# Causal convolution taps moved from TensorE to ScalarE and GpSimd in a two-layer hybrid block

## The chip, the cores and the metric

One core of a Trainium2 chip runs the whole kernel. The metric is the device time of one execution in microseconds, given as the median of several runs. The engines are TensorE (PE), VectorE (DVE), ScalarE (ACT), GpSimd (POOL) and the DMA queue of SyncE (SP). All of them run their own list of instructions in order and wait for each other through semaphores that are written out by hand.

## What is computed

The input is a sequence of 256 tokens with 1024 features. Two blocks of two layers each follow one another. The change touches the first block alone; its layer is, cut to what matters:

```python
a = rmsnorm(h, norm_mix_pre[i])
u = einsum('bsd,de->bse', a, w_in[i])
q, k, v, qi, ki, wi, u_conv, u_pool = split(u, IN_SPLITS)
# index scores: sum over 16 heads of relu(qi . ki) * wi; the 64 best keys of each token are kept
idx = einsum('bths,bth->bts', relu(einsum('bthd,bsd->bths', qi, ki)), wi) * idx_scale
_, sel = top_k(where(causal, idx, -inf), 64)
# softmax attention of 8 heads over the kept keys
# convolution branch, 256 channels, 31 causal taps
a, g = split(u_conv, 2)
y = a * sigmoid(g)
y = depthwise_conv(y, conv_dw, kernel=31) + conv_b
y = silu(layernorm(y, ln_g, ln_b)) @ conv_pw
# pooling branch: windowed means of 2, 4, 8, 16 tokens, minus the token, times pool_w, pool_scale
mix = concatenate([y_attn, y_conv, y_pool]) @ w_out
h = h + rmsnorm(mix, norm_mix_post)
# then a feed-forward part and a gated embedding
```

The second block (feed-forward, recurrent and retention mixer, feed-forward) is the same before and after.

## The kernel before

Weights arrive in chunks of 128 partitions by 2048 floats (1 MB), each as two half chunks of 1024 columns. SP loads a half chunk into one of two raw slots (`raw`) when VectorE has finished with the chunk two places earlier. ScalarE rounds it (`prep`, line 490, tile `whi`), VectorE subtracts to get the low part (`lo`, line 946, tile `wlo`), and TensorE multiplies three times (high by high, high by low, low by high). There are four places for such pairs, so ScalarE also waits until TensorE has released the chunk four places earlier. `prep(s)` and `lo(s)` stand at fixed places of their engines' lists and bring all chunks up to s.

A layer of the first block uses chunks 0 to 10 of its own for the input projection, and 11 to 14 for the output product. In the old order they are: 0 and 1 keys, values and index keys; 2 to 5 the index queries (`qi`), two of 8 heads each; 6 and 7 the queries (`q`); 8 and 9 the convolution's inputs and gates, one group of 128 channels each; 10 the pooling's input. The functions `block_in` (512 columns, 12 products for four feature tiles) and `pair_in` (256 columns, 24 products for a half chunk) do them, lines 1780 and 1826.

TensorE turns the projected tiles to feature-major form (`turn_in`, line 1797) once VectorE has applied the rotation (`rope`, line 1059); ScalarE copies the turned tiles out of PSUM (`turned_in`, line 573). Then come the index products (`dots`, line 1819), sixteen heads; two heads whose operands lie in different partition halves run side by side on TensorE when they are issued one after the other. ScalarE applies relu (line 590), VectorE multiplies by the weight and sums (`index_sums`, line 1084), three buffers deep. After the last head VectorE searches: eight rounds of MAX8 and MATCH_REPLACE8 (lines 1130, 1133). Then it copies the pooling input (line 1138), makes the additive mask `bias` (lines 1142 to 1145) and masks the scores of head after head (`masked`, lines 1152, 1156). ScalarE takes the exponential (line 637), TensorE turns the probabilities (`turn_probs`, 1889), ScalarE copies them (645), and TensorE multiplies by the values (`mix_values`, 1901 to 1905).

The convolution has two groups of 128 channels and 31 taps, 62 in all. Forty-six of them are done on TensorE (`taps`, line 1927): the product of a diagonal matrix of the tap's weights with the shifted input `YC`, in plain float32, which the trace records as two passes each. GpSimd makes the diagonals (line 415) in a ring of 16. The last 16 taps of group 1 are done by VectorE (`own_taps`, lines 1184, 1186) in the softmax stage, and added through one product with the identity (line 1945). TensorE does 14 taps before the first head and 7, 7, 6, 6, 6 after the first five. ScalarE then adds the convolution's bias (line 661); mean, variance and the scale follow as products with a constant matrix (lines 1951, 1966, 1975). GpSimd also does the pooling sums (lines 427 to 441) between two groups of diagonals. At the end the output product begins with the first half of the values (`tail`, line 1668, with `last_values` after one chunk).

At the start of the kernel, ScalarE and VectorE also make the sines of the rotation: VectorE `angles_by_feature` (line 1029) between `lo(2)` and `lo(3)`, ScalarE `sines` (line 521) after `prep(2)`.

## Time and profile before

| | us |
|---|---|
| median of 3 runs | 2367.45 |
| lowest, highest | 2366.25, 2367.78 |
| the profiled execution, its own time | 2367.65 |
| its span, first to last instruction | 2365.9 |
| TensorE busy | 2338.3 (99%) |
| VectorE busy | 1550.9 (66%) |
| ScalarE busy | 1195.0 (51%) |
| GpSimd busy | 119.3 (5%) |

Busy time is the time in which an engine has an instruction under way. Products overlap on TensorE, so what counts for its list is the distance from start to start. A timeline row gives the start, the time from the start of the first to the end of the last of the merged instructions, the engine, the line, what was written and read, the shape and the count, and in brackets the idle time before it with what ended it. The profile's lines are those of the kernel printed above.

### The profile page before, as it was taken

How to read it: one execution, taken by the hardware profiler on the slowest of the kernel's cores; microseconds unless marked ns; L12 is line 12 of the kernel's file. 1: busy time of each engine (PE TensorE's matmuls, PEld its weight loads, DVE VectorE, ACT ScalarE, POOL GpSimd, SP SyncE). 2: the span in 40 equal slices, each digit the busy share in tenths (PEclk: the TensorE clock that was granted, in tenths of full speed). 3: DMA queues.
4: the chain of work that ended last, by engine and by line, in shares of the span. 5: the costliest groups of instructions: out<-in, count | busy, mean ns of one | idle time of the engine just before them, and what ended most of it. 6: DMA issues, size and time to landing. Idle time of an engine off the chain costs nothing.

```text
span 2365.9 us, 30405 instructions
## 1 busy us (share of the span) xinstructions
PE 2338.3 (99%) x12096; PEld 1979.0 (84%) x12096; DVE 1550.9 (66%) x2041; ACT 1195.0 (51%) x1734; POOL 119.3 (5%) x223
## 2 busy tenths in 40 slices
PE   7999999999999999999999999999999999999998
PEld 6888888888888888988888888888889888888887
DVE  6866567866666656776485666665567765856664
ACT  6445446445455546546344455554465553444553
POOL 0500000500000000000000000000000000000000
PEclk9999999999999999999999999999999999999999
DMA  7236656236556665554656465565565455564553
GB/s 270 83 104 205 205 190 214 72 107 213 186 176 227 196 196 179 196 167 160 199 174 202 161 211 181 178 229 197 181 196 194 159 168 188 182 207 162 191 193 125
DMA packets 117501, 427.11 MB, mean 181 GB/s; under 512 B 13296, under 2 KB 13552, under 8 KB 117104
## 3 DMA queue, kind: packets, MB, share of 16 engines
q1 hardware_dynamic: 117360, 425.16, 54.4%
q8 instruction: 97, 1.59, 0.3%
q14 instruction: 44, 0.36, 0.0%
HBM read 424.05 MB, written 1.05 MB: 180 GB/s over the span
## 4 chain that ended last, share of the span: by engine, by line
PE 87%; DVE 6%; POOL 2%; DMA 1%; ACT 1%; issue 1%; SPq 0%; DVEq 0%; POOLq 0%; ACTq 0%
PE ub L1625 21%; PE ub L1626 11%; PE ub L1610 8%; PE ub L1612 8%; PE ub L1611 8%; PE acc L1610 8%; PE acc L1612 7%; PE acc L1611 7%; DVE wlo L946 2%; DMA raw<-in_w 1%; DVE XN L987 1%; PE acc L1927 1%; POOL tapd L415 1%; ACT junk L512 1%; PE acc L2040 1%
## 5 line engine op out<-in xcount | busy, mean ns | idle before, releaser
L946 DVE TENSOR_TENSOR wlo<-raw,whi 128x1024 fp32r<-128x1024 f32 x776 | 917.4, 1223 | 243.8 <-ACT whi L490 241.3
L490 ACT ACTIVATE whi<-raw 128x1024 fp32r<-128x1024 f32 x776 | 783.1, 1053 | 258.5 <-PE ub L1612 149.0
L1625 PE MATMUL ub<-xhl,whi 128*128 128x512 f32 x2176 | 770.3, 398 | 0.0
L1626 PE MATMUL ub<-xhl,wlo 128*128 128x256 f32 x2176 | 609.7, 280 | 0.0
L1625 PEld LDWEIGHTS ub<-xhl,whi 128*128 128x128 f32 x2176 | 408.6, 188 | 98.7 <-issue 0.5
L1626 PEld LDWEIGHTS ub<-xhl,wlo 128*128 128x128 f32 x2176 | 410.7, 189 | 2.4 <-issue 0.5
L1610 PE MATMUL acc<-whi,bhl 128*128 128x512 f32 x736 | 289.5, 393 | 0.0
L1612 PE MATMUL acc<-whi,bhl 128*128 128x512 f32 x736 | 287.1, 390 | 0.0
L1611 PE MATMUL acc<-wlo,bhl 128*128 128x512 f32 x736 | 286.8, 390 | 0.0
L1610 PE MATMUL ub<-whi,xhl 128*128 128x512 f32 (+1 forms) x704 | 275.4, 391 | 9.3 <-DVE wlo L946 5.0
L1612 PE MATMUL ub<-whi,xhl 128*128 128x512 f32 (+1 forms) x704 | 272.5, 387 | 0.0
L1611 PE MATMUL ub<-wlo,xhl 128*128 128x512 f32 (+1 forms) x704 | 272.3, 387 | 0.0
L1610 PEld LDWEIGHTS ub<-whi,xhl 128*128 128x128 f32 x704 | 132.7, 189 | 38.5 <-DVE wlo L946 7.2
L1612 PEld LDWEIGHTS acc<-whi,bhl 128*128 128x128 f32 x736 | 138.1, 188 | 29.9
L1610 PEld LDWEIGHTS acc<-whi,bhl 128*128 128x128 f32 x736 | 138.2, 188 | 29.0
L1611 PEld LDWEIGHTS acc<-wlo,bhl 128*128 128x128 f32 x736 | 138.3, 188 | 27.0
L1612 PEld LDWEIGHTS ub<-whi,xhl 128*128 128x128 f32 x704 | 132.6, 188 | 26.6
L1611 PEld LDWEIGHTS ub<-wlo,xhl 128*128 128x128 f32 x704 | 132.8, 189 | 25.3
L1348 DVE TENSOR_TENSOR tX<-tS,ub 128x512 f32<-128x512 f32 x72 | 49.5, 688 | 140.4 <-ACT tS L773 139.9
L773 ACT ACTIVATE tS<-ub 128x512 f32<-128x512 f32 x72 | 43.0, 597 | 154.3 <-PE ub L1626 154.1
L1610 PE MATMUL ub<-whi,bhl 128*128 128x512 f32 x256 | 99.8, 390 | 0.0
L1612 PE MATMUL ub<-whi,bhl 128*128 128x512 f32 x256 | 99.6, 389 | 0.0
(311 smaller groups left out, 2577.7 us busy)
## 6 DMA issues: line engine op xcount, KB each, us to landing
raw<-in_w SPq DMA_DIRECT2D x776, 512.0 KB, 4.8
gain<-in_gains SPq DMA_DIRECT2D x20, 512.0 KB, 8.1
par<-in_par SPq DMA_DIRECT2D x2, 1068.0 KB, 9.2
DEC<-in_decay SPq DMA_DIRECT2D x2, 768.0 KB, 7.5
H<-in_x SPq DMA_DIRECT2D x2, 512.0 KB, 6.2
out_h<-H SPq DMA_DIRECT2D x4, 256.0 KB, 2.3
par<-in_par SPq DMA_DIRECT2D x2, 419.0 KB, 7.9
PT<-in_p SPq DMA_DIRECT2D x2, 256.0 KB, 8.1
```

Of the source, the lines that this page charges most:

```text
L415: do(pool.tensor_scalar(tapd[:, n % TAP_RING, :], ident, par1[:, P1["dw"] + n:P1["dw"] + n + 1], 1.0, ALU.mult, ALU.mult), taps)
L490: do(act.activation(whi[:, s % RING, c], raw[:, s % RAW, c], ACT.Copy), counts["w_hi"])
L512: do(act.activation(junk[:, :], H[:, t, fcol(fb)], ACT.Square, scale=1.0 / 32, accum_out=ssh[:, t, fb:fb + 1]), counts["ssh"])
L773: do(act.activation(units(tS[:, j % 2, :]), ub[:, 2 * (j % 2):2 * (j % 2) + 2, 0:S], ACT.Copy), counts["a_out"])
L946: do(dve.tensor_tensor(wlo[:, s % RING, c], raw[:, s % RAW, c], whi[:, s % RING, c].bitcast(f32), ALU.subtract), counts["w_lo"])
L987: do(dve.scalar_tensor_tensor(XN[:, fcol(fb)], H[:, t, fcol(fb)], rh[:, t:t + 1], gain[:, 1, fcol(fb)], ALU.mult, ALU.mult), counts["xn_re ...
L1348: do(dve.tensor_tensor(units(tX[:, j % 2, :]), units(tS[:, j % 2, :]), ub[:, 2 * (j % 2):2 * (j % 2) + 2, S:2 * S], ALU.add), counts["us"])
L1610: pe.matmul(o, x_h, w_h, start=first, stop=False, skip_group_check=True)
L1611: pe.matmul(o, x_h, w_l, start=False, stop=False, skip_group_check=True)
L1612: return pe.matmul(o, x_l, w_h, start=False, stop=last, skip_group_check=True)
L1625: pe.matmul(bank, w_h, x.rearrange("p a n -> p (a n)"), start=first, stop=False, skip_group_check=True)
L1626: return pe.matmul(bank[:, S:], w_l, x[:, 0, :], start=False, stop=last, skip_group_check=True)
```

## The change

The 62 taps are divided anew. Group 0: tap 0 with the bias and all 30 others are made as products on ScalarE (`first_tap`, `tap_products`) and summed on GpSimd into `cacc`. Group 1: taps 0 to 10 are done that way too, tap 0 on ScalarE and ten as products on GpSimd itself; eight (11 to 18) stay on TensorE, with diagonals made early and kept apart (no ring); the last twelve stay on VectorE. ScalarE writes into a ring of four slots `prods` and waits for GpSimd's add of the product four places earlier. GpSimd adds group 0 alone for the first twenty products (256 elements) and both groups at once for the last ten (512 elements).

The chunks change places: 6 and 7 are the convolution's, 8 and 9 the queries, 10 the pooling's. The index products begin after the first half of chunk 4. The turn of the first index queries comes right behind that of the keys. The queries' rotation comes after the search, the pooling input's copy behind six of VectorE's own taps and chunk 11's low part. At the start chunks 3 and 4 are prepared ahead of the sines and `angles_by_feature`. Scores are issued two heads at a time. The pool product moves behind the last head, and the convolution's scale and output products move by some places in the output product.

```diff
-TAP_RING = 16
+TAP_RING = 4
-TAPS_DVE = 16
-TAPS_BEFORE, TAPS_AFTER = 14, (7, 7, 6, 6, 6)
+TAPS_POOL, TAPS_PE, TAPS_DVE = 11, 8, 12
+TAPS_BEFORE = 4
+TAP_ORDER = tuple(range(TAPS_POOL, TAPS)) + tuple(range(1, TAPS_POOL))
...
+        tapd = sb("tapd", 0, at=place[0], shape=[P, TAPS_PE, P])
+        prods = sb("prods", 0, at=unit(32), shape=[P, TAP_RING, 2, S])
...
GpSimd
-                    pool.wait_ge(sem["dots_done"], IDX_HEADS * (L + 1))
-                    early = TAP_RING + TAPS_BEFORE
-                    tap_diagonals(0, early)
+                    for n in range(TAPS_PE):
+                        c = P1["dw"] + TAPS + TAPS_POOL + n
+                        do(pool.tensor_scalar(tapd[:, n, :], ident, par1[:, c:c + 1], 1.0, ALU.mult, ALU.mult),
+                           counts["tap_ready"])
+                    for n, k in enumerate(TAP_ORDER):
+                        pool.wait_ge(sem["tap_made"], (TAPS + 1) * L + 1 + n + 1 + (k < TAPS_POOL))
+                        x = prods[:, n % TAP_RING, :, :]
+                        if k < TAPS_POOL:
+                            c = P1["dw"] + TAPS + k
+                            do(pool.tensor_scalar(x[:, 1, :], YC[:, 1, k:k + S], par1[:, c:c + 1], 1.0, ALU.mult, ALU.mult))
+                            settle()
+                            do(pool.tensor_tensor(cacc[:, :, :], cacc[:, :, :], x, ALU.add), counts["tap_used"])
+                        else:
+                            settle()
+                            do(pool.tensor_tensor(cacc[:, 0, :], cacc[:, 0, :], x[:, 0, :], ALU.add), counts["tap_used"])
                     nxt("pool_in")
...
-                    tap_diagonals(early, 2 * TAPS - TAPS_DVE)
...
ScalarE
                 prep(2)
                 sines_by_token()
+                prep(4)
                 sines()
...
+                    def first_tap(f):
+                        act.wait_ge(sem["in_free"], 3 * L + f + 1)
+                        act.wait_ge(sem["par_in"], 16 * (L + 1))
+                        do(act.activation(cacc[:, f, :], YC[:, f, 0:S], ACT.Identity,
+                                          bias=par1[:, P1["conv_b"] + f:P1["conv_b"] + f + 1],
+                                          scale=par1[:, P1["dw"] + f * TAPS:P1["dw"] + f * TAPS + 1]), counts["tap_made"])
+                    def tap_products(first, end):
+                        for n in range(first, end):
+                            if n == TAPS - TAPS_POOL:
+                                first_tap(1)
+                            if n >= TAP_RING:
+                                act.wait_ge(sem["tap_used"], (TAPS - 1) * L + n - TAP_RING + 1)
+                            k = TAP_ORDER[n]
+                            do(act.activation(prods[:, n % TAP_RING, 0, :], YC[:, 0, k:k + S], ACT.Copy,
+                                              scale=par1[:, P1["dw"] + k:P1["dw"] + k + 1]), counts["tap_made"])
...
+                    prep(s0 + 7)
                     turned_in(0)
+                    turned_in(1)
+                    relus(0, 2)
                     prep(s0 + 8)
+                    relus(2, 5)
                     copy(2, 0)
                     copy(2, 1)
-                    turned_in(1)
+                    relus(5, 8)
                     prep(s0 + 9)
-                    relus(0, 4)
+                    turned_in(2)
+                    sigmoid(0)
+                    relus(8, 11)
+                    first_tap(0)
+                    tap_products(0, 4)
                     prep(s0 + 10)
-                    turned_in(2)
-                    relus(4, 10)
+                    relus(11, 14)
+                    tap_products(4, 6)
+                    sigmoid(1)
+                    relus(14, 16)
+                    tap_products(6, 10)
                     prep(s0 + 11)
+                    tap_products(10, 14)
                     copy(3, 0)
+                    tap_products(14, 18)
                     copy(3, 1)
-                    relus(10, 13)
-                    sigmoid(0)
-                    relus(13, 16)
                     prep(s0 + 12)
-                    sigmoid(1)
-                    prep(s0 + 13)
+                    tap_products(18, 24)
                     turned_in(3)
+                    tap_products(24, TAPS - 1)
...
VectorE
-                lo(2)
+                lo(4)
                 angles_by_feature()
-                lo(3)
...
+                    rope(1)
+                    lo(s0 + 7)
+                    index_sums(0, 2)
                     lo(s0 + 8)
+                    index_sums(2, 5)
                     rope(2)
+                    index_sums(5, 8)
                     lo(s0 + 9)
-                    index_sums(0, 4)
-                    lo(s0 + 10)
-                    index_sums(4, 10)
-                    lo(s0 + 11)
-                    rope(3)
-                    index_sums(10, 16)
                     dve.wait_ge(sem["pads_ready"], L + 1)
                     gated(0)
+                    index_sums(8, 11)
+                    lo(s0 + 10)
+                    index_sums(11, 14)
+                    gated(1)
+                    index_sums(14, 16)
...
-                        if r == 3:
-                            gated(1)
-                    used(s0 + 10)
-                    do(dve.tensor_copy(UP[:, :, 16:], units(acc[:, 2, :])), counts["in_free"])
...
+                    rope(3)
                     settle()
                     do(dve.tensor_scalar(bias[:, :], cur, TAKEN, OFF, ALU.not_equal, ALU.mult))
...
+                    lo(s0 + 11)
+                    dve.wait_ge(sem["par_in"], 16 * (L + 1))
+                    own_taps(TAPS - TAPS_DVE, TAPS - TAPS_DVE + 6)
+                    used(s0 + 10)
+                    do(dve.tensor_copy(UP[:, :, 16:], units(acc[:, 0, :])), counts["in_free"])
...
                     masked(0)
                     masked(1)
                     lo(s0 + 12)
                     for hh in range(HEADS):
                         if hh + 2 < HEADS:
                             masked(hh + 2)
-                        if hh < 4:
+                        if hh < 3:
+                            k0 = TAPS - TAPS_DVE + 6 + 2 * hh
+                            own_taps(k0, k0 + 2)
...
+                        if hh == 5:
+                            nxt("conv_done")
+                            dve.wait_ge(sem["tap_used"], (TAPS - 1) * (L + 1))
+                            do(dve.tensor_tensor(cacc[:, 1, :], cacc[:, 1, :], acc[:, 3, S:2 * S], ALU.add), counts["c_ready"])
...
TensorE
-                    both(2, 0)
+                    block_in(2, 0, 0)
                     turn_in(0)
-                    both(2, 1)
                     turn_in(1)
-                    block_in(3, 0, 0)
+                    give(block_in(2, 0, 1))
                     dots(0, 2)
+                    give(block_in(2, 1, 0), "xz")
+                    dots(2, 5)
+                    give(block_in(2, 1, 1))
+                    dots(5, 8)
+                    pair_in(s0 + 6, 2, 0)
                     turn_in(2)
+                    pair_in(s0 + 6, 2, 1)
+                    dots(8, 11)
+                    pair_in(s0 + 7, 0, 0)
+                    dots(11, 14)
+                    pair_in(s0 + 7, 0, 1)
+                    dots(14, 16)
+                    for part in range(2):
+                        both(3, part)
+                    pair_in(s0 + 10, 0, 0)
                     turn_in(3)
+                    pair_in(s0 + 10, 0, 1)
...
                     scores(0)
                     scores(1)
-                    taps(TAPS_BEFORE)
+                    taps(0, TAPS_BEFORE)
                     for hh in range(HEADS):
                         turn_probs(hh)
-                        if hh + 2 < HEADS:
+                        if hh % 2 == 0 and hh + 2 < HEADS:
                             scores(hh + 2)
+                            scores(hh + 3)
                         if hh:
                             mix_values(hh - 1)
-                        if hh < len(TAPS_AFTER):
-                            taps(TAPS_AFTER[hh])
+                        if hh < TAPS_PE - TAPS_BEFORE:
+                            taps(TAPS_BEFORE + hh, TAPS_BEFORE + hh + 1)
...
                     mix_values(HEADS - 1)
+                    pe.wait_ge(sem["par_in"], 16 * (L + 1))
+                    nxt("pool_out")
...
```

## Rows read from the trace of the kernel before

**Rows 1.** Windows: us; busy of PE, PEld, DVE, ACT, POOL; PEclk, DMA share, GB/s

```profile
...
427.50:441.10 13.60, 13.60 (x104) 12.79 (x103) 12.74 (x54) 4.53 (x6) 5.41 (x15) 1.00 0.01 2
441.10:476.90 35.80, 34.89 (x193) 28.32 (x193) 31.70 (x56) 14.97 (x46) 23.91 (x35) 1.00 0.28 89
...
```

**Rows 2.** Timeline of PE, second layer: start us, duration us, what [idle before]

```profile
...
457.60 2.17 PE L1927 MATMUL acc<-YC,tapd 128*128 128x256 f32 x8 [0.91 <-POOL tapd L415]
...
461.60 2.81 PE L1927 MATMUL acc<-YC,tapd 128*128 128x256 f32 x12
464.25 0.49 PE L1889 MATMUL ub<-cst,sm 128*128 128x128 f32 x3
...
476.93 0.48 PE L1610 MATMUL acc<-whi,bhl 128*128 128x512 f32 x1
...
```

**Rows 3.** Timeline of DVE, second layer, index sums to the first scores

```profile
...
424.11 2.60 DVE L1084 SCALAR_TENSOR_TENSOR iacc<-sm,wi,iacc 128x128 f32<-128x128 f32 x6 [0.46 <-ACT sm L590]
...
427.30 0.62 DVE L1130 MAX8 best<-iacc 128x8 f32<-128x128 f32 x2
...
428.74 0.62 DVE L1130 MAX8 best<-work 128x8 f32<-128x128 f32 x2
...
439.22 0.68 DVE L1138 COPY UP<-acc 128x512 f32<-128x512 f32 x1
...
441.11 0.56 DVE L1152 SCALAR_TENSOR_TENSOR sm<-ub,bias 128x384 f32<-128x384 f32 x1
...
443.55 2.35 DVE L946 TENSOR_TENSOR wlo<-raw,whi 128x1024 fp32r<-128x1024 f32 x2
```

**Rows 4.** Timeline of DVE, second layer, softmax stage

```profile
...
448.00 2.88 DVE L1186 SCALAR_TENSOR_TENSOR CD<-YC,par,CD 128x256 f32<-128x256 f32 x3
...
459.73 2.09 DVE L1186 SCALAR_TENSOR_TENSOR CD<-YC,par,CD 128x256 f32<-128x256 f32 x4
...
471.29 0.61 DVE L1156 TENSOR_REDUCE rmax<-sm 128x1 f32<-128x128 f32 x2
...
```

**Rows 5.** Timeline of POOL, second layer, softmax stage

```profile
...
446.73 1.08 POOL L427 TENSOR_TENSOR W<-UP 128x542 f32<-128x542 f32 x1
...
449.05 0.69 POOL L431 TENSOR_TENSOR W<-W 128x265 f32<-128x265 f32 x1
...
457.01 8.84 POOL L415 TENSOR_SCALAR tapd<-cst,par 128x128 f32<-128x128 f32 x16
```

**Rows 6.** Tile tapd: min/median/max ns of one, first and last start

```profile
...
L415 POOL TENSOR_SCALAR tapd<-cst,par x92: 366/374/2509, 76.7 to 464.5; 128x128 f32<-128x128 f32 x92
...
```

**Rows 7.** Timeline of PE, second layer: turns of keys and of index queries

```profile
...
390.93 0.60 PE L1804 MATMUL ub<-cst,Z 128*128 128x128 f32 x4
...
396.86 1.03 PE L1811 MATMUL ub<-cst,ZA 128*128 128x128 f32 x8
...
```

**Rows 8.** Timeline of DVE, second layer: end of their rotation

```profile
...
390.88 0.43 DVE L1077 TENSOR_TENSOR ZA<-tX 128x256 f32<-128x256 f32 x1
...
```

**Rows 9.** Timeline of PE, second layer: conv half chunk, products of 256 columns

```profile
...
415.45 0.28 PE L1617 MATMUL acc<-xhl,whi 128*128 128x256 f32 x1
...
415.81 0.28 PE L1617 MATMUL acc<-xhl,whi 128*128 128x256 f32 x1
...
```

**Rows 10.** Timeline of PE, start of the kernel

```profile
...
15.41 0.48 PE L1612 MATMUL ub<-whi,xhl 128*128 128x336 f32 x1
...
16.96 0.32 PE L1612 MATMUL ub<-whi,xhl 128*128 128x336 f32 x1
...
31.48 0.50 PE L1610 MATMUL ub<-whi,xhl 128*128 128x512 f32 x1 [1.79 <-DVE wlo L946]
...
```

**Rows 11.** Timeline of DVE, first layer: angles, then lo of chunk 3

```profile
...
24.96 0.35 DVE L1033 TENSOR_SCALAR ang<-posf,cst 128x256 f32<-128x256 f32 x1
...
30.20 2.36 DVE L946 TENSOR_TENSOR wlo<-raw,whi 128x1024 fp32r<-128x1024 f32 x2 [1.74 <-ACT whi L490]
...
```

135 lines of the change are left out of this document (47 added, 88 removed).

## The prediction

> **What bounds the kernel now.** The page says TensorE 99% busy, so I read first where the change works: two stretches, one in each layer of the first block (about 37 to 129 us and 385 to 477 us), that repeat almost to the tenth. The windows [rows 1] show in the second layer 13.6 us of search in which TensorE is always busy and VectorE 12.74 of 13.6, and then a softmax stage of 35.8 us with TensorE at 34.9 and VectorE at 31.7. So TensorE ends last, but VectorE has only 4.1 us to spare in that stage. Next, TensorE's timeline [rows 2]: six taps (12 records, two passes each) fill 461.60 to 464.25, so a tap is 0.442 us; once TensorE waits 0.91 us for a tap's diagonal; the output product starts at 476.93. Then VectorE's timeline [rows 3]: three heads of index sums in 2.45 us (0.82 a head, 2.60 with GpSimd at work), search from 427.30, one round in 1.44, its end where the pool copy begins at 439.22, masks from 441.11, two of them in 2.44 (1.24 with gaps), one chunk's low part in 2.35. In the stage itself [rows 4] four of its own taps take 2.09 (0.52 each) and the last reduction ends at 471.90, 5.0 before the output product.
>
> **What TensorE loses.** 38 of 46 taps a layer go: 38 x 0.442 = 16.8 us, with the 0.91 wait 17.7, twice 35.4. Scores by pairs spare single-head products as well; I price them at nothing, because VectorE's list covers them, and if that cover went they would add to the gain. This saving counts only as far as the others follow, so the sum goes by them.
>
> **What GpSimd gets.** Twenty adds of 256 elements, ten more of 512, each of those with a product of 256. An add of 542 takes 1.08, one of 265 takes 0.69 [rows 5]: 1.4 ns an element on 0.31, so 0.68 and 1.04, plus 0.08 between dependent ones. The product of 256 is not in the trace; a 128-wide one takes 0.374 [rows 6], so between that and twice it; I take 0.50, nearest to the same start-up plus twice the data. Sum 20 x 0.76 + 10 x 1.70 = 32 us, and then the pooling, 10.3 (446.73 to 457.01). From the first product at 413 this ends by about 469 with its waits, before the pool product near 479: its length is covered by search and softmax. ScalarE's 32 products (a 256-wide one about 0.4) lie in its idle time, but its ring of four slots ties it to the adds: the first exponential stands behind product 30, so behind add 26. I put that at 450.3, and with 1.3 of table load at 452 where its mask is ready at 450.7. Small, and VectorE's low part covers it. VectorE's new wait for add 30 stands ahead of the mean's subtraction and the values' low part; the adds end near 458.5 and it comes at 473.7, so it costs nothing, and the two copies of ScalarE that it replaces (0.8) were waiting time. No DMA is added; SP's queue keeps its order.
>
> **What GpSimd takes from VectorE.** One diagonal took 2.51 instead of 0.37 [rows 6], beside two low parts; three VectorE taps beside GpSimd's adds took 2.88 instead of 1.56 [rows 4, 5]. But four taps beside diagonals of 0.54 each were not slowed (2.09) [rows 4, 5]. So operations of VectorE with two SBUF inputs and GpSimd's exclude each other, and only while data move (1.4 ns an element on GpSimd, about 1 ns on VectorE); the start-up overlaps. Masks, reductions and search rounds beside GpSimd kept their times. The Trainium skill, "SBUF — State Buffer", "SBUF: two separate sides", has it that the shared pair of ports is locked for the whole instruction and the other engine blocks fully. The unslowed four taps speak against the whole length; by whole locks I would get about 22 us more instead of 7.
>
> **The second layer, step by step.** I wrote the engines' lists side by side, each step starting where the one ahead of it and its wait end. The same table for the old order gives search at 427.6 and masks at 441.5, within 0.4 of the rows.
> Head: the queries' turn is now right behind the keys' turn; that was 6 us earlier (390.93 to 396.86, two blocks of 2.72 between) [rows 7]. Its rotation ends at 391.3 [rows 8], because two low parts stand ahead. TensorE, there at 388.8, waits 2.5.
> Dots: behind the last dot stood two convolution half chunks (48 products every 0.12, 5.8 us [rows 9]) too many, now four query blocks: the pool's and the turn are common, so dots end 10.9 - 5.8 = 5.1 earlier less the 2.5: 2.6 earlier, 421.5.
> Index sums: eight heads, chunk 10's low part and the second gate now run against the adds; I count 2.7 of exclusion. Search starts at 425.9, 1.4 early, and ends 11.5 later at 437.4, since a gate is no longer in it.
> Then, ahead of the masks: the query rotation 1.35 (formerly while VectorE waited for dots), bias 1.05, low part 2.35, six taps 3.3, pool copy 0.85, together 8.9, and 3.0 of exclusion: first mask at 449.3, 8.2 later than 441.11. The scores are there at 444, so TensorE then stands idle.
> Stage: VectorE's masks 8 x 1.24 = 9.9, three low parts 7.1, six taps 3.1, the first half's division 1.1, exclusion 3.1: 24.3 to the last reduction (30.8 in the old order). Then exponential, last two heads, mean, square and variance products and now the pool product: 6.2 against 5.0. Output product at 479.8, **2.9 late**. TensorE's idle time there is some 19 us, in gaps of 7, 4.5 and 3.5.
>
> **The first layer.** Moving chunks 3 and 4 ahead of the angles removes the 1.79 wait [rows 10]: chunk 3 came behind the angles, begun at 24.96, at 30.20 [rows 11]. But the angles (3.9) now stand behind chunk 4's low part, which waits for its load and ends near 32; then sines, the copies and the first rotation end near 38.7, and the second one, behind chunk 5, at 42.4. TensorE waits 1.1 for the keys' turn, 3.2 for the queries', and 2.4 before the first dots, since ScalarE copies the turned data behind chunk 7: 6.7 for 1.8 and 0.6 now. Dots end as before; search starts about 0.5 later, the masks 10 later (103.1 for 93.4), and the stage is 5.9 shorter: **4.3 late**. The other chunks' order leaves each queue's load count as it was, loads one chunk behind their old place in the search are not needed before the output product: nothing.
>
> **Sum and median.** +2.9 + 4.3 = +7.2. The clock: after 7 us without work some of TensorE's next products may run at the lower level. At the start a 336-wide one takes 0.48, once it has worked 0.32 [rows 10]; the granted-clock column reads 1.00 in the stage now [rows 1], so no row shows a fall. Between 0 and all products of the stage doubled (5.5 a layer on the chain, and 1.4 on the output's first products) I take 1 a layer, as most of them wait for VectorE anyway. Total +9.2. The profiled execution took 2367.65 (span 2365.9 and 1.7 around it), 0.2 over the median 2367.45. Forecast **2377 us**. I call 0.2%, 4.7 us, what a measurement can tell.
>
> **Rivals.**
> 1. Forecast, 2377: VectorE is the stage's bound; chance 0.40, of which 0.16 within 0.2%.
> 2. Faster. The exclusion costs VectorE nothing and the head's turns find their rotations done. My count without these gives -4.9 in the second layer and -3.5 in the first: **2359**. For it: VectorE drops four taps a layer (2.1 us) and TensorE's 35 us are real. Against: three taps in 2.88. It decides if VectorE's delays fall under 5 us of my 8.8 a layer. Chance 0.26, 0.02 of it within 0.2%.
> 3. GpSimd is the bound: adds 30% dearer in data (0.87 for 256, toward the 0.79 of contended ones and beyond) put the exponentials behind the ring, +4.7 a layer: **2386**, chance 0.12.
> 4. TensorE falls to 1.2 GHz through the stage: 6.9 a layer on 7.2, **2388**, chance 0.16, 0.02 within. For it: gaps of 7 us. Against: work between them. The Trainium skill, "TensorE: Matmul & The Clock Gate", "What's actually happening", says an idle array is put back to half rate; no row here shows it after warm work.
> 5. Exclusion for whole instructions: +9.7 and +12.6 from my table so locked, **2390**, chance 0.06; the old order would then be some 13 us a layer slower than it is.
>
> The range: 2360 to 2392 leaves out about half of rival 2 and the tails of 4 and 5. Faster 0.24, the same 0.16 + 0.02 + 0.02 = 0.20, slower 0.56.
>
> **What the profile would show.** Right: TensorE's busy time in each softmax stage near 18 of 30 us, gaps before the first transposed head, first masks near 103 and 449, VectorE's low parts and taps slower than 1.18 and 0.52, waits before both first turns. Wrong: first masks before 445, or TensorE's gaps ended by GpSimd, or index sums beside adds at 0.82 a head, or a granted clock below 1.00 in the stage.

## The result, and the profile after

The kernel before took 2366.99 us (median of 6, 2366.2 to 2367.8), the changed one **2387.09** (median of 6, 2384.3 to 2391.0): ratio 1.0084, 95% interval 1.0074 to 1.0094, so 20 us slower. The forecast was 2377, in a range from 2360 to 2392. The profiled execution is the fastest of its six (2384.3, span 2382.5 for 2365.9), so the trace shows 16.6 us of those 20.

Where they are, by the starts on the timelines of VectorE and TensorE, in us (S first round of the search, M first mask, R last reduction, O output product):

| | S to M | M to R | R to O | S to O |
|---|---|---|---|---|
| before, both layers | 13.8 | 30.2 | 5.6 | 49.6 |
| after, first layer | 26.2 | 24.6 | 7.6 | 58.4 |
| after, second layer | 26.2 | 24.3 | 7.8 | 58.3 |
| forecast, second layer | 23.4 | 23.7 | 6.8 | 53.9 |

The search starts 0.9 later in the first layer (80.53 for 79.64) and, counted from the output product before it, 1.9 earlier in the second. So 0.9 + 8.8 = 9.7 in the first layer and 8.6 - 1.9 = 6.7 in the second: 16.4, nearly all there is. Behind the second output product both kernels take 1889 us. The 0.9 and the 1.9 are those of this one trace. In two kernels further down (e2, e4) the instructions ahead of each search, the head of the layer, are the same as here, and there the first search starts at 82.5 and 82.0, and the second comes 298.9 and 298.4 after the output product, for 296.1 here. Three traces of the old head (before, e6, e10) agree within 0.3 us: 79.3 to 79.6 and 298.0. So the new head varies by up to 2.0 us in the first layer and 2.8 in the second, and this trace, the fastest, flatters it. In e2's second layer ScalarE waits 2.08 us for a half chunk (1.05 here), VectorE's rotation of the first index queries stands behind that half chunk's low part, and TensorE waits for the rotation and then turns at the lower level. The turn in the changed kernel and in e2:

```profile
400.21 1.09 PE L1843 MATMUL ub<-cst,ZA 128*128 128x128 f32 x8 [1.65 <-DVE ZA L1104]
```

```profile
402.35 1.97 PE L1843 MATMUL ub<-cst,ZA 128*128 128x128 f32 x8 [2.93 <-DVE ZA L1104]
```

Windows of the changed kernel, second layer (columns as in [rows 1]):

```profile
435.00:447.00 12.00, 9.62 (x54) 8.27 (x52) 11.34 (x50) 9.59 (x20) 9.29 (x14) 1.00 0.00 1
461.00:494.00 33.00, 25.79 (x125) 20.79 (x126) 26.85 (x50) 17.00 (x47) 19.10 (x17) 0.69 0.30 96
```

TensorE is no longer full in either window, and its granted clock in the stage is 0.69: stretches at 1.2 GHz. The page's first part has VectorE 13 us and ScalarE 25 us busier, GpSimd 45, TensorE 14 less.

VectorE's timeline from the end of the search to the first mask (start, duration, what); where one instruction stands alone it was looked at in a narrow window:

```profile
446.10 0.41 DVE L1160 MATCH_REPLACE8 work<-best,work 128x256 f32<-128x256 f32 x1
446.62 0.46 DVE L1100 TENSOR_TENSOR tX<-ZA,cc 128x256 f32<-128x256 f32 x1
447.00 1.34 DVE L1101 TENSOR_TENSOR tX<-ZA,ss 128x128 f32<-128x128 f32 x1
...
449.12 1.31 DVE L1164 TENSOR_SCALAR bias<-work 128x384 f32<-128x384 f32 x1
...
451.04 3.44 DVE L974 TENSOR_TENSOR wlo<-raw,whi 128x1024 fp32r<-128x1024 f32 x2
454.59 0.35 DVE L1206 TENSOR_SCALAR CD<-YC,par 128x256 f32<-128x256 f32 x1
454.98 1.40 DVE L1208 SCALAR_TENSOR_TENSOR CD<-YC,par,CD 128x256 f32<-128x256 f32 x1
456.41 0.58 DVE L1208 SCALAR_TENSOR_TENSOR CD<-YC,par,CD 128x256 f32<-128x256 f32 x1
457.03 1.37 DVE L1208 SCALAR_TENSOR_TENSOR CD<-YC,par,CD 128x256 f32<-128x256 f32 x1
458.44 0.58 DVE L1208 SCALAR_TENSOR_TENSOR CD<-YC,par,CD 128x256 f32<-128x256 f32 x1
459.05 1.37 DVE L1208 SCALAR_TENSOR_TENSOR CD<-YC,par,CD 128x256 f32<-128x256 f32 x1
460.34 0.68 DVE L1215 COPY UP<-acc 128x512 f32<-128x512 f32 x1
...
461.26 0.56 DVE L1174 SCALAR_TENSOR_TENSOR sm<-ub,bias 128x384 f32<-128x384 f32 x1
```

and GpSimd's in the same stretch:

```profile
450.86 1.40 POOL L428 TENSOR_TENSOR cacc<-cacc,prods 128x512 f32<-128x512 f32 x1
452.24 2.51 POOL L426 TENSOR_SCALAR prods<-YC,par 128x256 f32<-128x256 f32 x1
454.83 1.27 POOL L428 TENSOR_TENSOR cacc<-cacc,prods 128x512 f32<-128x512 f32 x1
456.08 0.65 POOL L426 TENSOR_SCALAR prods<-YC,par 128x256 f32<-128x256 f32 x1
456.81 1.31 POOL L428 TENSOR_TENSOR cacc<-cacc,prods 128x512 f32<-128x512 f32 x1
458.10 0.65 POOL L426 TENSOR_SCALAR prods<-YC,par 128x256 f32<-128x256 f32 x1
458.83 1.31 POOL L428 TENSOR_TENSOR cacc<-cacc,prods 128x512 f32<-128x512 f32 x1
```

Lay the two side by side. The tap begun at 454.98 meets an add that lasts to 456.10 and ends 0.28 after it: 1.40 instead of 0.58. The next one meets a product and is not slowed; the one after it meets the next add, 1.37. And the other way round: GpSimd's product at 452.24 waits for the second piece of the low part, which ends at 454.48, and takes 2.51. So each engine stands still for most of the other's instruction, but for some 0.3 of start-up. The product shows it best: it began before VectorE's second piece (453.27), which passed it and was not slowed.

TensorE's timeline, the waits ahead of the query heads' turn, the first and the third transposed head, and the output product:

```profile
449.14 1.97 PE L1843 MATMUL ub<-cst,ZA 128*128 128x128 f32 x8 [4.52 <-DVE ZA L1104]
...
463.54 0.90 PE L1921 MATMUL ub<-cst,sm 128*128 128x128 f32 x3 [5.49 <-ACT sm L672]
...
470.88 0.81 PE L1921 MATMUL ub<-cst,sm 128*128 128x128 f32 x3 [2.02 <-ACT work L680]
...
493.31 0.58 PE L1642 MATMUL acc<-whi,bhl 128*128 128x512 f32 x1
```

The turn of eight took 1.97 here and 1.03 in [rows 7], the three transposes 0.81 to 0.90 for 0.49 [rows 2]: that is the lower level, behind waits of 4.5 and 5.5 us.

### The profile page after: what moved, and what is told of

The parts are those of the page before. It is cut to its first block, busy times and chain, and to the rows that moved or that the text cites. A ratio compares the mean times of both kernels' runs of the same rounds, so it can differ in the third digit from the quotient of the medians.

```text
span 2382.5 us, 30199 instructions
## 1 busy us (share of the span) xinstructions
PE 2323.9 (98%) x11944; PEld 1966.6 (83%) x11944; DVE 1564.2 (66%) x2035; ACT 1220.3 (51%) x1794; POOL 164.1 (7%) x227
## 3 DMA queue, kind: packets, MB, share of 16 engines
HBM read 424.05 MB, written 1.05 MB: 178 GB/s over the span
## 4 chain that ended last, share of the span: by engine, by line
PE 84%; DVE 10%; ACT 2%; DMA 2%; POOL 1%; issue 1%; DVEq 0%; SPq 0%; POOLq 0%; ACTq 0%
PE ub L1657 21%; PE ub L1658 11%; PE ub L1642 8%; PE ub L1644 8%; PE ub L1643 8%; PE acc L1642 7%; PE acc L1644 7%; PE acc L1643 7%; DVE wlo L974 3%; DMA raw<-in_w 2%; DVE CD L1208 1%; DVE XN L1015 1%; ACT whi L496 1%; ACT junk L518 1%; PE acc L2073 1%
## 5 line engine op out<-in xcount | busy, mean ns | idle before, releaser
L391 POOL TENSOR_SCALAR vy<-ssy 128x1 f32<-128x1 f32 x20 | 6.6, 332 | 1625.6 <-ACT junk L510 1625.6
L1642 PE MATMUL ub<-whi,bhl 128*128 128x512 f32 x256 | 99.8, 390 | 0.0
```

Source lines behind the costliest of these rows:

```text
L1642: pe.matmul(o, x_h, w_h, start=first, stop=False, skip_group_check=True)
```

## The experiments

The times in the first column are medians of 4 to 11 runs; the kernel before ran beside each of them at 2367.4 to 2367.7. All other columns are from one execution each, the profiled one, whose own time is in the second column and can lie some us from the median. The last column but one, the head, is the start of the first search and the time from the first output product to the second search. The other starts are those above, first / second layer:

| kernel | us | profiled | S to M | M to R | R to O | S to O | head | mean clock |
|---|---|---|---|---|---|---|---|---|
| before | 2367.0 | 2367.7 | 13.8 / 13.8 | 30.2 / 30.2 | 5.6 / 5.6 | 49.6 / 49.6 | 79.6 / 298.0 | 1.000 |
| after | 2387.1 | 2384.3 | 26.2 / 26.2 | 24.6 / 24.3 | 7.6 / 7.8 | 58.4 / 58.3 | 80.5 / 296.1 | 0.986 |
| e1 short adds | 2371.1 | 2369.2 | 20.0 / 20.0 | 24.7 / 23.6 | 9.5 / 7.0 | 54.3 / 50.6 | 78.9 / 294.4 | 0.990 |
| e2 TensorE filled | 2384.9 | 2387.1 | 26.3 / 26.3 | 24.3 / 24.3 | 6.7 / 6.7 | 57.2 / 57.2 | 82.5 / 298.9 | 0.995 |
| e3 ten taps to TensorE | 2377.1 | 2375.1 | 21.4 / 21.2 | 23.8 / 23.0 | 7.4 / 6.7 | 52.6 / 50.8 | 81.3 / 299.5 | 0.992 |
| e4 late taps | 2391.7 | 2393.4 | 21.2 / 20.7 | 32.3 / 32.4 | 7.3 / 8.1 | 60.8 / 61.1 | 82.0 / 298.4 | 0.983 |
| e6 before, eight taps | 2370.5 | 2370.2 | 14.5 / 14.5 | 28.8 / 28.8 | 8.0 / 7.5 | 51.3 / 50.8 | 79.3 / 298.0 | 0.987 |
| e7 turn later | 2387.6 | 2387.7 | 26.2 / 26.2 | 24.6 / 24.6 | 8.4 / 8.7 | 59.2 / 59.5 | 82.9 / 295.1 | 0.987 |
| e8 ring untied | 2372.3 | 2369.7 | 20.6 / 21.1 | 23.3 / 23.0 | 6.7 / 6.7 | 50.6 / 50.7 | 80.7 / 297.3 | 0.994 |
| e9 products on ScalarE | 2377.2 | 2377.6 | 23.4 / 22.3 | 24.0 / 24.0 | 6.7 / 7.9 | 54.0 / 54.2 | 82.0 / 296.7 | 0.992 |
| e10 eight taps, filled | 2376.6 | 2376.2 | 14.5 / 14.5 | 34.0 / 34.0 | 5.6 / 5.6 | 54.2 / 54.2 | 79.5 / 298.0 | 1.000 |
| e11 head | 2371.5 | 2372.5 | 21.6 / 21.5 | 23.2 / 23.2 | 6.7 / 6.7 | 51.4 / 51.4 | 78.7 / 300.3 | 0.992 |
| e12 late copy | 2372.2 | 2376.0 | 20.3 / 22.3 | 23.5 / 24.0 | 6.0 / 9.8 | 49.8 / 56.0 | 79.6 / 299.2 | 0.992 |
| e13 filled, the best | 2368.4 | 2370.2 | 19.6 / 22.1 | 22.7 / 22.7 | 7.5 / 6.0 | 49.8 / 50.8 | 80.4 / 298.0 | 0.997 |

**What the sums on GpSimd cost.**

```diff
-do(pool.tensor_tensor(cacc[:, :, :], cacc[:, :, :], x, ALU.add), counts["tap_used"])
+do(pool.tensor_tensor(cacc[:, :, 0:1], cacc[:, :, 0:1], x[:, :, 0:1], ALU.add), counts["tap_used"])
```

(the same for the add of one half and for GpSimd's product)

> The kernel after, in which GpSimd's thirty sums and ten products of the convolution work on one column instead of 256 (most of the convolution's sum is left out); every wait and every other instruction stays. Theory A, GpSimd's data phases cost VectorE its time: between the search's end and the first mask VectorE took 14.7 us where its operations alone would take 8.9, and in the stage its low parts and taps took 2.8 more than alone; so 8.4 us a layer come back, 2387 becomes about 2370, and the first masks come at about 101 and 450. Theory B, the order of work and the clock are what costs: VectorE's operations get shorter but the time stays over 2380. A time below 2366 would say that the sums cost more than their exclusion (the exponentials tied to them).

2371.11 (2367.6 to 2375.1), ratio to before 1.0017 [1.0008, 1.0026]: 16 of the 20 us came back, theory A's figure. Between the two profiled executions it is 15.1: 11.8 from S to O and 3.4 in the heads. The index sums no longer meet adds there, but 3.4 is also no more than what the heads vary by. VectorE's timeline from the search's end to the first mask in this kernel:

```profile
438.63 0.41 DVE L1160 MATCH_REPLACE8 work<-best,work 128x256 f32<-128x256 f32 x1
...
439.48 0.29 DVE L1101 TENSOR_TENSOR tX<-ZA,ss 128x128 f32<-128x128 f32 x1
...
440.46 0.36 DVE L1164 TENSOR_SCALAR bias<-work 128x384 f32<-128x384 f32 x1
...
441.30 2.35 DVE L974 TENSOR_TENSOR wlo<-raw,whi 128x1024 fp32r<-128x1024 f32 x2
...
444.14 2.59 DVE L1208 SCALAR_TENSOR_TENSOR CD<-YC,par,CD 128x256 f32<-128x256 f32 x5
...
447.56 0.56 DVE L1174 SCALAR_TENSOR_TENSOR sm<-ub,bias 128x384 f32<-128x384 f32 x1
```

The same list is 8.5 long (439.04 to 447.56) that took 14.7 beside the adds (446.51 to 461.26): 6.2 a layer in this stretch alone. The stage itself did not get shorter in the first layer (24.7) and little in the second (23.6), because the pooling now ran beside its first taps (pairs at 1.90 and 1.89, not shown) and TensorE stood at the lower level for much of it (a granted clock of 0.65 and 0.78 from M to O, R to O 9.5 and 7.0).

**What TensorE's lower level costs the changed kernel.** Identity products where TensorE waits, which nobody reads:

```diff
+for _ in range(30):
+    pe.transpose(ub[:, 2, 0:P], ident, ident)
 turn_in(3)
...
 for hh in range(HEADS):
+    if hh in (0, 2, 4):
+        fill_idle(42 if hh == 0 else 14)
     turn_probs(hh)
```

> The kernel after, with products of the identity on TensorE (30 ahead of the query heads' turn, 42 ahead of the first transposed head, 14 ahead of the third and of the fifth) where it otherwise waits; their results are never read. It should hold the granted clock at 1.00 through both softmax stages. Theory A, VectorE's list sets the stage and the clock costs 1 us a layer, in the tail behind the last reduction: about 2385. Theory C, the 1.2 GHz stretches are the missing 7 us and more: 2375 to 2379, with TensorE's products at their full rate. If the added products stand in the way of work, the gaps' ends get later and it is 2389 or more.

2384.88 (4 runs, 2384.6 to 2387.1), 2.2 below the changed kernel, as theory A had it, though with the changed kernel's runs 6.7 apart the medians alone would not show it. In the traces S to O is 57.2 for 58.3 and 58.4, nearly all of it behind the last reduction (6.7 for 7.6 and 7.8). The profiled execution as a whole is 2.8 slower, since its heads took 2.0 and 2.8 longer. M to R did not move by more than 0.3: there TensorE has room even at 1.2 GHz. The clock did not stay at 1.00 everywhere (0.995 in the mean for 0.986), so 1.1 a layer is the least that the level costs.

**Where VectorE's taps should be.**

```diff
-TAPS_POOL, TAPS_PE, TAPS_DVE = 11, 8, 12
-TAPS_BEFORE = 4
+TAPS_POOL, TAPS_PE, TAPS_DVE = 11, 18, 2
+TAPS_BEFORE = 12
...
-own_taps(TAPS - TAPS_DVE, TAPS - TAPS_DVE + 6)
...
```

> The kernel after, with ten of VectorE's twelve taps as products on TensorE (18 there, 2 on VectorE; 10 more diagonals for GpSimd before the first gate). TensorE has some 19 us idle per stage and 10 taps are 4.4 us. VectorE loses six taps of about 1 us ahead of the masks and four of 0.6 to 1.1 in the stage. Theory A (VectorE's list is the bound until the exponentials meet GpSimd's ring): masks are ready 6 us earlier, but the last product on ScalarE still waits for GpSimd's adds, so the first exponential moves by 1 us or less, and only the stage gets shorter: 4 to 5 us a layer, about 2378. If the ring does not hold it: 9 us a layer, 2369. Rival, TensorE's idle time is no room (the taps sit in the wrong places): 2384 or more.

2377.07 (8 runs, 2370.5 to 2384.0), as expected: S to M 5 us shorter, and then the ring holds. ScalarE's timeline in this kernel, and VectorE's first reduction, done at 455.84, after it:

```profile
454.59 0.51 ACT L625 ACTIVATE prods<-YC,par 128x256 f32<-128x256 f32 x1 [3.19 <-POOL cacc L433]
456.40 0.51 ACT L625 ACTIVATE prods<-YC,par 128x256 f32<-128x256 f32 x1 [1.30 <-POOL cacc L433]
458.21 0.51 ACT L625 ACTIVATE prods<-YC,par 128x256 f32<-128x256 f32 x1 [1.30 <-POOL cacc L433]
458.74 1.28 ACT L677 ACT_TABLE_LOAD   x1
460.03 0.40 ACT L677 ACTIVATE sm<-sm,rmax 128x128 f32<-128x128 f32 x1
```

```profile
455.23 0.61 DVE L1183 TENSOR_REDUCE rmax<-sm 128x1 f32<-128x128 f32 x2
```

The mask was ready 4.2 before its exponential (3.9 in the first layer): three products wait for three adds ahead of it. VectorE then waited 2.1 for TensorE's third scores, which stand behind that exponential.

**Taps behind the masks instead.** The six own taps and the low part of chunk 11 move behind the first masks, three taps behind each of heads 0 to 3.

```diff
-lo(s0 + 11)
-own_taps(TAPS - TAPS_DVE, TAPS - TAPS_DVE + 6)
...
-if hh < 3:
-    k0 = TAPS - TAPS_DVE + 6 + 2 * hh
-    own_taps(k0, k0 + 2)
+if hh < 4:
+    k0 = TAPS - TAPS_DVE + 0 + sum((3, 3, 3, 3)[:hh])
+    own_taps(k0, k0 + (3, 3, 3, 3)[hh])
```

> The kernel after, with VectorE's first six own taps and the low part of chunk 11 moved from ahead of the first masks to behind them (three taps behind each of the heads 0 to 3). Theory A: the first mask is ready 9 us earlier, but the exponentials stand behind GpSimd's ring (the last product on ScalarE at about 460 in the second layer) and VectorE's list keeps its length, so the end moves by 1 us or less a layer: 2385 to 2388. Rival, the late first mask itself is the cost (TensorE could work in the gap): 4 us a layer, 2379.

2391.72, 4 above the forecast's upper end. The order bought nothing, as expected, and lost what I had not seen. From the waits of VectorE in this kernel's second layer (who waited for whom: us in total, times, longest):

```profile
DVE UP L1213 <- PE acc L1649: 3.6, 1, 3.6
```

The taps had covered the time in which TensorE, held up by the query turn, makes the pool chunk that VectorE copies next.

**TensorE's saving by itself.** The kernel before, without 38 of its 46 taps and their diagonals:

```diff
-TAPS_BEFORE, TAPS_AFTER = 14, (7, 7, 6, 6, 6)
+TAPS_BEFORE, TAPS_AFTER = 4, (1, 1, 1, 1)
+TAP_LIST = [(0, 0)] + [(1, k) for k in range(7)]
...
-    early = TAP_RING + TAPS_BEFORE
+    early = 8
...
-tap_diagonals(early, 2 * TAPS - TAPS_DVE)
```

> The kernel before, in which TensorE does 8 taps a layer instead of 46 and GpSimd makes 8 diagonals (38 taps are left out of the convolution's sum; nothing takes their place). It prices TensorE's saving by itself. Theory A, the saving counts only as far as VectorE follows: from the first mask to the output product VectorE's list is 9.9 of masks, 7.1 of low parts, 8.4 of its sixteen taps, 1.1 for the division and about 1 of exclusion, 27.5, plus 5.6 behind the last reduction, 33.1 for 35.8 now: 2.7 us a layer, about 2362, less what a lower clock costs. Rival, TensorE's 16.8 us a layer count in full: 2334. Between, about 2350, if TensorE's load also delayed VectorE.

2370.46, ratio 1.0013 [1.0004, 1.0022]: the work was only taken away, and the kernel was slower, where theory A said 2362. Its window from the first mask to the output product of the second layer:

```profile
443.00:479.40 36.40, 32.76 (x122) 24.55 (x122) 29.82 (x57) 14.86 (x46) 8.68 (x8) 0.58 0.26 87
```

M to R fell from 30.2 to 28.8, R to O rose from 5.6 to 7.5 and 8.0, at a clock of 0.58 for 1.00 [rows 1]. TensorE with 38 of its taps gone is still 32.8 of 36.4 busy, since what is left takes nearly twice as long: with the taps out, the engine gets its first waits, and the lower level then fills it again.

The clock is only part of that loss. S to M is 14.5 for 13.8, and it is 14.5 as well in the next kernel, at a clock of 1.000. With most of the diagonals gone, GpSimd begins the pooling earlier, and its first add meets VectorE's mask. VectorE's instruction in the kernel before, and in this one beside GpSimd's add:

```profile
440.46 0.34 DVE L1144 TENSOR_TENSOR bias<-bias,cst 128x128 f32<-128x128 f32 x1
```

```profile
441.46 1.25 POOL L428 TENSOR_TENSOR W<-UP 128x542 f32<-128x542 f32 x1 [12.11 <-DVE small L1140]
...
441.80 1.06 DVE L1144 TENSOR_TENSOR bias<-bias,cst 128x128 f32<-128x128 f32 x1
```

From S to O the two layers together are 2.8 longer: 1.4 are this meeting, 4.2 the tails, and a gain of 2.8 from M to R stands against them.

**The same with TensorE kept busy.**

```diff
 taps(TAPS_BEFORE)
+fill_idle(36)
...
 taps(TAPS_AFTER[hh])
+fill_idle(16)
```

> The kernel before with 8 taps on TensorE and 38 left out (2370.5, its softmax stages at a granted clock of 0.50 to 0.72), now with identity products in their places that nobody reads: 36 ahead of the first transposed head and 16 behind each of the first five heads, about 2 us a head where the taps took 2.7. Theory C2, the lower level is what turned that kernel's saving into a loss: the clock stays at 1.00, the tail behind the last reduction falls from 7.5 back to 5.6, the stage gets to VectorE's list, so 2362 to 2364, faster than the kernel before. Rival, the loss has nothing to do with the clock (VectorE's own work is what is longer): 2370 again.

2376.58: a miss, because the filling was too much. TensorE's timeline of this kernel:

```profile
445.79 6.64 PE L1881 MATMUL acc<-cst 128*128 128x128 f32 x58
...
454.07 3.73 PE L1881 MATMUL acc<-cst 128*128 128x128 f32 x32
```

Sixteen took 3.7 us, more than the 2.7 of the taps they stood for, so M to R became 34.0 with TensorE full. It does show that the tail's loss is the clock: at 1.000 it is 5.6 again, and S to M stays at 14.5. Whether the thinned kernel would reach 2362 at the upper level stays open; I have no run with the right amount of filling.

**The head's order.**

```diff
-turn_in(1)
 give(block_in(2, 0, 1))
+turn_in(1)
```

> The kernel after with one move: the first query turn stands behind the second block of chunk 4 (2.7 us of products) instead of ahead of it. TensorE waited 3.15 us for it in the first layer and 1.65 in the second. If these waits are on the path to the search (TensorE's products end last before it): the search starts 1.5 to 2.5 earlier in the first layer and 1 to 1.5 in the second, and everything behind keeps its length, 2383 to 2385. Rival: VectorE's index sums beside GpSimd's adds end last, the search starts where it did, 2387.

2387.63 (4 runs, 2386.2 to 2389.8), level with the changed kernel. The second search came 1.0 earlier, counted from the output product before it; the first came 2.3 later and the tails 0.8 to 0.9 longer. The heads vary by as much without any edit (80.5 to 82.5, and 296.1 to 298.9), and the runs lie 4 to 7 us apart, so the 2 us looked for cannot be told; inconclusive.

**The ring untied** (on top of the ten taps):

```diff
-tap_products(24, TAPS - 1)
+tap_products(24, 27)
 exps(0)
+tap_products(27, 28)
 for hh in range(HEADS):
     if hh + 1 < HEADS:
         exps(hh + 1)
+    if hh < 2:
+        tap_products(28 + hh, 29 + hh)
```

> The kernel with ten of VectorE's taps on TensorE (2377), with ScalarE's last three tap products behind the first, second and third pair of exponentials instead of ahead of them all. There the first exponential came 5.1 us after its mask, behind GpSimd's adds. Theory A: it now comes 1.2 after the first mask, and the stage starts up to 5 us earlier; VectorE's operations run beside the adds for longer (1 to 2 us back), so 3 us a layer, about 2371. Rival, GpSimd's last sums become the bound at the mean (they end at 115 and 467, the mean's product is at 129 and 480): below 1 us a layer, 2375 or more.

2372.32, ratio 1.0020 [1.0011, 1.0030]; the first exponential 1.2 behind its mask in both layers (101.29 to 102.53, 449.59 to 450.83), so the ring no longer holds it. The median is 4.8 lower, 2.4 a layer of the 3 forecast, but the traces do not put that in the stage. S to O fell by 2.0 in the first layer and by 0.1 in the second, where M to R is 23.0 in both kernels. VectorE's wait for scores went from 2.1 to 1.2, and two of its low parts took 3.40 and 3.31 us beside the adds, for 3.31 and 2.55. The other 3 us between the two profiled executions are in the heads. What the traces place in the two stages is 2 us in all.

**The ten products on ScalarE** (on top of that):

```diff
+if k < TAPS_POOL:
+    do(act.activation(prods[:, n % TAP_RING, 1, :], YC[:, 1, k:k + S], ACT.Copy,
+                      scale=par1[:, P1["dw"] + TAPS + k:P1["dw"] + TAPS + k + 1]))
...
-do(pool.tensor_scalar(x[:, 1, :], YC[:, 1, k:k + S], par1[:, c:c + 1], 1.0, ALU.mult, ALU.mult))
```

> The previous kernel with the second half's ten tap products on ScalarE (0.42 us each) instead of GpSimd (0.65 each with its gap, one of them 2.5). GpSimd's pace for these ten taps falls from 2.0 to about 1.4 us each, its sums end some 7 us earlier, and VectorE's low part and taps meet less of it. Theory A: 1 to 2 us a layer beside the previous kernel, 2367 to 2369, level with the kernel before. Rival: ScalarE's extra 4.2 us stand ahead of the exponentials and take it back, 2371 or more.

2377.16, 4.8 slower, a miss. GpSimd's timeline of this kernel:

```profile
444.13 5.56 POOL L431 TENSOR_TENSOR cacc<-cacc,prods 128x512 f32<-128x512 f32 x4
452.08 4.60 POOL L431 TENSOR_TENSOR cacc<-cacc,prods 128x512 f32<-128x512 f32 x3 [2.40 <-ACT prods L626]
458.06 3.90 POOL L431 TENSOR_TENSOR cacc<-cacc,prods 128x512 f32<-128x512 f32 x2 [1.38 <-ACT prods L626]
```

The first four adds now follow each other without the product between them, exactly beside VectorE's rotation, three of whose four operations took 1.35 to 1.42 where one did in the previous kernel; then GpSimd stands empty behind ScalarE, which waits 3.4 for the query turn that this rotation holds up. Products between the adds were VectorE's gaps; that this is the whole loss is argued, not tested. It was not the rival that I had named: the first exponential starts at 456.20, with the end of its mask's reduction.

**Smaller repairs.** The chunk between the angles taken back:

```diff
-prep(4)
+prep(3)
...
-lo(4)
+lo(3)
```

> The kernel with ten taps on TensorE and the last three products behind exponentials (2372), with chunk 4 taken out from between the two sets of angles: only chunk 3 stands ahead of the second angles and the sines. In the first layer the angles stood behind chunk 4's low part, and TensorE waited 2.3, 3.2 and 2 us for turned data. Theory A: these waits get 1.5 to 2.5 shorter, once: 2370. Rival, TensorE then waits for chunk 4's low part behind the angles (as for chunk 3 in the kernel before, 1.8): 2372 or more.

2371.47 (2367.8 to 2375.3), 0.9 below; the keys' turn 1.5 earlier (38.94 for 40.48) and the first search 2.0 earlier, but S to M came out 0.4 to 1.0 longer and the second search 3.1 later. Within the spread; no more than the earlier turn is shown.

> The previous kernel with the pool copy behind the first two masks (VectorE waited 0.7 us for it there) and the pool's product ahead of the variance product instead of behind the last head. GpSimd takes the pool up only behind its sums, so the later copy delays nothing; the product (1.1 us) then stands where TensorE waits 0.5 us for ScalarE's squares. Theory: 0.7 and 0.5 to 1 a layer, 2 to 3 in all below the previous kernel, 2367 to 2368. Rival: the pool's result is not ready there (it ends at 474.7, the squares' product is at about 476 in the second layer), TensorE waits for GpSimd, and it is level or slower.

```diff
+masked(0)
+masked(1)
 used(s0 + 10)
 do(dve.tensor_copy(UP[:, :, 16:], units(acc[:, 0, :])), counts["in_free"])
...
-masked(0)
-masked(1)
```

(and the pool's product moved ahead of the variance product)

2372.24, from 2366.4 to 2376.0: no gain in the median. But its profile holds a good and a bad layer of one program, S to O 49.8 and 56.0. Windows from the last third of the first and of the second stage (they do not hold just the same products):

```profile
120.00:130.00 10.00, 10.00 (x61) 9.11 (x61) 6.25 (x16) 4.23 (x13) 5.18 (x7) 0.83 0.31 106
...
470.00:480.00 10.00, 10.00 (x44) 8.59 (x43) 5.23 (x12) 4.18 (x14) 4.30 (x4) 0.50 0.33 105
```

TensorE is full in both: 61 products at a clock of 0.83, 44 at 0.50. The ten runs of this kernel go with the mean clock: 0.996 in the fastest, 0.992 in the slowest (correlation -0.90; -0.96 in the eight runs of e3, from 2370.5 at 0.995 to 2384.0 at 0.989). Which of the two is cause a correlation does not say; the next kernel tests it.

**All of it, with TensorE's waits filled.**

```diff
+pe.wait_ge(*U_[1].free)
+for _ in range(14):
+    pe.transpose(ub[:, 1, 0:P], ident, ident)
 turn_in(1)
...
+for _ in range(34):
+    pe.transpose(ub[:, 2, 0:P], ident, ident)
 turn_in(3)
...
 for hh in range(HEADS):
+    for _ in range(8 if hh == 2 else 4 if hh == 4 else 0):
+        pe.matmul(acc[:, 3, 0:P], ident, ident, start=False, stop=False, skip_group_check=True)
     turn_probs(hh)
```

> The previous kernel (2372.2, runs from 2366.4 to 2376.0; in its profile the first layer takes 49.8 us from the search to the output product at a clock mostly 1.00 and the second 56.0 with 0.50 in its last third), with products of the identity where TensorE waits: 14 ahead of the first query turn (1.6 us), 34 ahead of the query heads' turn (3.9 of a 4.5 us wait), 8 of two passes ahead of the third transposed head (1.9 of 2.3) and 4 ahead of the fifth (0.9 of 1.3). Theory C3: the spread of these kernels is where TensorE's lower level falls; with the waits filled the clock stays at 0.998 or more, both layers take 49.5 to 50.5, and it is 2367 to 2369 with runs within 3 us, level with the kernel before. Rival: the spread comes from elsewhere (the head, the loads), the median stays at 2371 or more.

2368.37 (11 runs, 2365.8 to 2372.5), ratio to before 1.0005 [0.9996, 1.0014]: the median as forecast and level with the kernel before, 18.7 below the changed one and 3.9 below e12. The rest of theory C3 was met in part: the spread of 6.7 us is wider than the 3 forecast (e12 had 9.6), the clock is 0.996 to 0.999 and not 0.998 or more, and the runs still go with it (correlation -0.83): the waits are filled for the most part, not wholly. No version beat the kernel before by more than can be measured.

## Why the prediction was right in sign and short by ten

**Right.** The bound moved to VectorE as forecast, and the order of the steps held: from search to mask GpSimd and the moved work, then a stage of 24.3 and 24.6 between the starts (23.7 forecast), 5.6 to 5.9 shorter than before. Without the adds the list between search and masks is 8.5 (e1), for which I had 8.9. Small adds beside index sums: six in 3.03 where six alone take 2.45. The first exponential was not held by the ring in the changed kernel itself: its mask's reduction is done at 462.45, the exponential starts at 462.50, the table was loaded by 461.98. The clock's term of 1 us a layer is 1.1 (e2). The tail was right with it: behind the last reduction's end I had 6.2, and it is 6.05 in e2 and 7.0 and 7.2 in the changed kernel.

**Near by luck.** The search is 1.9 early in the second layer (1.4 forecast) and 0.9 late in the first (0.5), but in the fastest execution only: with the same head e2 and e4 have it 0.9 and 0.4 late in the second layer, 2.9 and 2.3 in the first. I had priced the loads at nothing, and the second layer's new head waits for one.

**Wrong, the main term: "exclude each other, and only while data move".** This is the step of the sum that failed, by its size. I put 3.0 ahead of the masks; it is 6.2 (e1 against the changed kernel), in both layers: 6.4 of the missing 10 us (of 7.4 in the profiled execution). Three things were in it. The exclusion covers nearly the whole instruction, as the product of 2.51 behind two pieces shows; for the adds, data alone would give nearly the same, once they have their true length. Operations of VectorE with one SBUF input were not free of it: the bias took 1.31 for 0.36. And the adds are dearer than my line through [rows 5] gave: 0.74 for 0.68, and 1.31 for 1.04 (median of 40 and of 20), so that a tap's add blocks longer. The trace of the kernel before had a row of that very size, which I passed over for a line through two others:

```profile
455.70 1.33 POOL L441 TENSOR_TENSOR PO<-PO,UP 128x512 f32<-128x512 f32 x1
```

The four unslowed taps of [rows 4] misled me: there GpSimd made diagonals of one input. Such a product, at 0.65 for 0.48, leaves a tap at 0.58 where an add makes it 1.40. Whether it gives way or is only short enough to fit into the start-ups, no run separates. The Trainium skill, "SBUF — State Buffer", "SBUF: two separate sides", has an exclusive lock for the whole instruction, taken by whichever starts first, and counts VectorE's two-port modes among its takers beside operations with two SBUF inputs; the rows of taps and bias agree with it within the 0.3 of start-up. The product agrees in that it is shut out, but not in the order: it started at 452.24, ahead of the second piece of the low part (453.27), and ended behind it. My rival 5 had this rule, at 2390 and a chance of 0.06; its sum was near (2387) and its chance much too low.

**Rival 4 (1.2 GHz through the stage) half happened.** The granted clock from the first mask to the output product was 0.64 and 0.69, which my text named as a wrong sign, and TensorE was busy for 25 of 32 us where I had 18 of 30; but the stage is VectorE's, so it cost 1.1 a layer and not 6.9. What I had not thought of is its place in the *before* side of the sum: I wrote that the saving "counts only as far as the others follow" and took it as zero or more. Taken alone it is a loss of 3 us (e6): a TensorE with its first waits falls to the lower level, which costs 4.2 in the two tails, and the pooling that moves up takes 1.4 more from VectorE. The Trainium skill, "TensorE: Matmul & The Clock Gate", "What's actually happening", has only the two levels and an idle array put back to the lower; the rows agree in both (turn of eight 1.03 and 1.97).

**Rival 3 (GpSimd the bound)** lay right behind: its price for the add was met for 512 elements (1.31 for 1.04), but the late masks hid it. It held the first exponentials as soon as VectorE was relieved (e3, 3.9 and 4.2 a layer), and one reordering let them go (e8); but S to O got only 2.0 and 0.1 shorter by that, so it was hardly the bound even there. **Rival 2** is out: its condition was less than 5 of exclusion a layer.

Of the profiled 16.6, then, 12.4 are the exclusion ahead of the masks (e1), 2.2 the clock (e2, from one trace each, at least), and the rest is the net of the moved list, the shorter stage and the head, which I can add up from the timelines but did not separate by a run. The 3.1 of exclusion that I had put into each stage is not separated either: in e1 the pooling took the adds' place there. The other 3.4 to the median of 2387.1 are spread between runs (2384.3 to 2391.0); the kernel before spread 1.5 to 3.2. In e3, e12 and e13 the spread goes with the mean clock; in the six runs of the changed kernel, all at 0.985 or 0.986, it does not. Its cause is open; the heads, which are 4.8 and 3.8 longer in e2 and e4 than in the changed kernel's fastest execution, are where I would look first, but one execution of each was profiled. Scores by pairs were priced at nothing and not tried alone.

## What to carry to other kernels

Price work on GpSimd by what it takes from VectorE, instruction by instruction on two timelines laid side by side: an add of 1.3 us beside VectorE operations of 0.5 costs each that it meets about 0.8. Move work off a full engine only if another one's list gets shorter by it: here ten taps put back from VectorE to TensorE were worth 10 us, and 38 taken from TensorE were worth less than nothing. Look also at what moves up when work goes: the pooling, set free of the diagonals, met VectorE's mask. An engine that the throttle watches should either be full or have its waits filled, and once it has waits, compare kernels by many runs.

## What the runs showed of the hardware that I had not expected

- GpSimd's add of two SBUF operands takes 0.74 us for 256 elements a partition and 1.31 for 512, where its pooling add of 265 takes 0.69 [rows 5].
- A GpSimd product (0.48 alone) that meets a low part of VectorE takes 2.5, and 0.65 beside VectorE's taps.
- VectorE's search rounds and masks kept their times beside all of it: a round is 1.44 in both kernels, the mask 0.56.
- A GpSimd product that began at 452.24 was passed by the second piece of VectorE's low part, which began at 453.27 and took its usual 1.2 us.
- Work taken out of a full TensorE made the kernel 3 us slower (2370.5 for 2367.5), at a clock of 0.58 in the stage for 1.00; 1.4 us of it were GpSimd's pooling against VectorE's mask.
